# Three layers of attention, retention and gated FFN on one core: a ring of six half-size weight slots, and the modulation vector summed in single steps

## The reference, cut to what matters

```python
# layer 1 (even): differential attention, 8 heads ("A"); gated short conv; cross attention to mem, 4 heads ("X")
u = rms_norm(h, norm_g); proj = u @ e_w_in                      # 1024 x 7168
h = h + concat(ya*silu(az), yb*silu(bz), yx*silu(xz)) @ e_w_out # 2048 x 1024
# layer 2 (odd): forgetting attention, 12 heads ("C"); cross attention, 4 heads ("X")
u = rms_norm(h, norm_g); proj = u @ o_w_in                      # 1024 x 7180
h = h + concat(yc*silu(cz), yx*silu(xz)) @ o_w_out
# layer 3: adaptive modulation, grouped-query attention beside retention, then a gated FFN
mod_x = silu(c) @ w_mod + b_mod      # one vector of 6 * 1024 = 12 chunks of 512
mod_c = silu(c_ctx) @ w_mod + b_mod  # only its first 4 chunks are used
sh_m, sc_m, gt_m, sh_f, sc_f, gt_f = split(mod_x, 6)
hx = rms_norm(x)*(1+sc_m) + sh_m;  hc = rms_norm(ctx)*(1+csc_m) + csh_m
x  = x + gt_m * rms_norm(mix(hx, hc), g_post_mix)
hf = rms_norm(x)*(1+sc_f) + sh_f
x  = x + gt_f * rms_norm(swiglu(hf), g_post_ffn)
```

## Time and profile before

| | |
|---|---|
| median of 3 runs | 1060.45 us (1054.36 to 1062.51) |
| profiled execution, whole | 1062.14 us |
| its span, first to last instruction | 1060.3 us |
| granted TensorE clock over the span | 0.952 of full |
| TensorE busy | 946.7 us (89%) |
| VectorE busy | 702.9 us (66%) |
| ScalarE busy | 475.7 us (45%) |
| GpSimd busy | 66.7 us (6%) |
| moved by DMA | 174.55 MB, 165 GB/s in the mean |

### The profile page before, as it was taken

The page is one execution under the profiler, slowest core; times in us unless marked ns, Lnnn a source line. Parts: engine busy times, 40 slices in busy tenths (PEclk is TensorE's granted clock), DMA queues, the critical chain, the costliest instruction groups (busy, mean ns, idle before and its releaser), DMA issues. The chain is left out here.

```text
span 1060.3 us, 14368 instructions
## 1 busy us (share of the span) xinstructions
PE 946.7 (89%) x5572; PEld 820.6 (77%) x5572; DVE 702.9 (66%) x1058; ACT 475.7 (45%) x800; POOL 66.7 (6%) x63
## 2 busy tenths in 40 slices
PE   4999987999798899999999897987789679999996
PEld 3788866989676778888879676775578579999885
DVE  4567878878777745667686766647745657755643
ACT  4455554544333336555555434434543434333541
POOL 0201110000000010101010000100000000000000
PEclk9999998999899889999999989989999879999999
DMA  7544456665566354545454664341222326663660
GB/s 261 168 150 159 142 177 193 206 225 170 197 216 205 122 187 148 181 158 180 158 187 154 219 227 145 103 158 57 80 80 80 130 89 239 238 199 120 221 215 40
DMA packets 89348, 174.55 MB, mean 165 GB/s; under 512 B 4269, under 2 KB 8770, under 8 KB 89282
## 3 DMA queue, kind: packets, MB, share of 16 engines
q1 hardware_dynamic: 86656, 166.78, 47.1%
q0 software_dynamic: 1888, 6.25, 1.8%
q10 hardware_dynamic: 738, 0.61, 0.2%
HBM read 172.57 MB, written 1.06 MB: 164 GB/s over the span
## 5 line engine op out<-in xcount | busy, mean ns | idle before, releaser
L1570 DVE TENSOR_TENSOR wlo<-raw,whi 128x1024 fp32r<-128x1024 f32 (+2 forms) x278 | 323.5, 1177 | 164.2 <-ACT whi L1287 163.3
L1287 ACT CAST whi<-raw 128x1024 fp32r<-128x1024 f32 (+2 forms) x278 | 276.5, 1010 | 203.6 <-PE acc L987 73.6
L996 PE MATMUL acc<-xhi,whi 128*128 128x256 f32 x736 | 215.1, 292 | 9.6 <-DVE slo L1588 4.5
L997 PE MATMUL acc<-xhi,wlo 128*128 128x256 f32 x736 | 210.1, 285 | 0.0
L998 PE MATMUL acc<-xlo,whi 128*128 128x256 f32 x736 | 210.0, 285 | 0.0
L985 PE MATMUL acc<-whi,xhi 128*128 128x512 f32 (+2 forms) x368 | 151.3, 411 | 11.9 <-DVE xlo L1588 4.6
L996 PEld LDWEIGHTS acc<-xhi,whi 128*128 128x128 f32 x736 | 143.0, 194 | 13.0 <-issue 5.3
L987 PE MATMUL acc<-whi,xlo 128*128 128x512 f32 (+2 forms) x368 | 144.5, 393 | 0.0
L986 PE MATMUL acc<-wlo,xhi 128*128 128x512 f32 (+2 forms) x368 | 144.3, 392 | 0.0
L997 PEld LDWEIGHTS acc<-xhi,wlo 128*128 128x128 f32 x736 | 143.2, 195 | 0.7 <-issue 0.5
L998 PEld LDWEIGHTS acc<-xlo,whi 128*128 128x128 f32 x736 | 143.0, 194 | 0.0
(11 more groups left out here) (291 smaller groups left out, 1179.1 us busy)
## 6 DMA issues: line engine op xcount, KB each, us to landing
raw<-in_e_w_in SPq DMA_DIRECT2D x28, 1024.0 KB, 5.3
raw<-in_o_w_in SPq DMA_DIRECT2D x28, 1024.0 KB, 5.1
raw<-in_w_mod SPq DMA_DIRECT2D x24, 1024.0 KB, 5.1
raw<-in_w_ffn_in SPq DMA_DIRECT2D x20, 1024.0 KB, 5.5
raw<-in_w_in SPq DMA_DIRECT2D x14, 1024.0 KB, 5.2
raw<-in_w_ffn_out SPq DMA_DIRECT2D x10, 1024.0 KB, 5.1
raw<-in_e_w_out SPq DMA_DIRECT2D x8, 1024.0 KB, 6.0
raw<-in_o_w_out SPq DMA_DIRECT2D x8, 1024.0 KB, 5.2
```

The source lines that it names most:

```text
L996: mm(o, wh, hi, start=a, stop=False, skip_group_check=True)
L997: mm(o, wl, hi, start=False, stop=False, skip_group_check=True)
L1287: nc.scalar.copy(whi[:, s.i % SPLIT_SLOTS, 0:s.nk, 0:n], raw[:, s.raw.i % RAW_SLOTS, s.koff:s.koff + s.nk, 0:n]).then_inc(S["hi_ready"], 1)
L1570: tt(wlo[:, slot, 0:s.nk, 0:n], raw[:, s.raw.i % RAW_SLOTS, s.koff:s.koff + s.nk, 0:n], whi[:, slot, 0:s.nk, 0:n].bitcast(F32), ALU.subtra ...
```

## The change

The raw ring becomes six slots of 512 KB instead of three of 1 MB: the same bytes of SBUF, twice the loads, each issued when the load six before it is read. Each k-tile of the modulation is a step of its own. A chunk with `c_ctx` takes one k-tile at every second position (two VectorE instructions), one without it a k-tile at every position (one instruction), both with rank 3, behind all other steps of the position. `mod_out` stands two positions behind the last k-tile, and VectorE's part of it (`mod_take`) one position later, ahead of that position's other steps. The chunks with `c_ctx` (0 to 3) start at position 12 and end at 82, and are followed by none until 100; chunks 4 to 9 are placed from 100 to 148; 10 and 11 stay at 216 to 232. Chunks without `c_ctx` take the halves of `macc` in turn. The gate chunks 4, 5, 10, 11 go the way of the others to columns in `modc`, with the bias from the columns; later (positions 152 to 156, and 236 to 240) VectorE multiplies the identity by the four columns into `macc`, which is the chunk on four diagonals (`gate_diag`), and one matmul of all ones spreads it to all rows of `tp` (`gate_rows`). The bias DMA of GpSimd and the one-row addition are gone.

```diff
-RAWK = 4
-RAW_SLOTS, SPLIT_SLOTS, LEAD = 3, 4, 3
+RAWK = 2
+RAW_SLOTS, SPLIT_SLOTS, LEAD = 6, 4, 3
...
-    def mod(self, pos, chunk, ctx=False, gate=False):
-        pos = max(pos, self.pos) + max(pos, self.pos) % 2
...
+    def mod(self, pos, chunk, ctx=False):
+        pos = max(pos, self.pos)
+        stride = 2 if ctx else 1
+        def read(k):
+            st = self.step("mod", chunk=chunk, u=k // RAWK, part=k % RAWK, ctx=ctx, prev=self.count.get("mod_read", 0),
+                           after=self.count.get("mod_ps", 0))
             self.tick(st, "mod_read")
+            done.append(st.on["mod_read"])
...
+            st = self.step("mod_out", chunk=chunk, ctx=ctx, mod_read=done[-1])
             self.tick(st, "mod_ps", "mod_sb")
-            self.uses(st, "tp" if gate else "o", "mod_sb")
+            self.uses(st, "o", "mod_sb")
             self.chunks.append(chunk)
-        for i in range(4):
-            self.at(pos + (i if ctx else i // 2 * 2), lambda i=i: read(i // 2, i % 2))
-        self.at(pos + 6, out, 2)
-        return pos + 8
+            self.at(self.pos + 1, lambda: self.step("mod_take", first=st), -2)
+        last = pos + (KT - 1) * stride
+        for k in range(KT):
+            self.at(pos + k * stride, lambda k=k: read(k), 3)
+        self.at(last + 2, out, 2)
+        return last + (4 if ctx else 1)
+
+    def gate_row(self, pos, chunk):
...
+        self.at(pos, diag, 2)
+        self.at(pos + 1, rows, 2)
+        return pos + 3
...
     b = heads("A", "g0", evs, pl.pos, 4, 0)
+    m = pl.pos
+    for chunk in range(4):
+        m = pl.mod(m, chunk, ctx=True)
...
-    m = pl.pos
-    for chunk in (6, 7, 8, 9, 0, 1, 2, 3):
-        m = pl.mod(m, chunk, ctx=chunk < 4)
...
     b = heads("X", "g1", evs, pl.pos, 4, 12, gain="ox")
+    m = max(m, pl.pos + 4)
+    for chunk in range(4, 10):
+        m = pl.mod(m, chunk)
...
-    pl.mod(pl.mod(pl.pos + 4, 4, gate=True), 5, gate=True)
+    pl.gate_row(pl.gate_row(pl.pos + 4, 4), 5)
...
-    pl.mod(pl.mod(pl.pos + 8, 10, gate=True), 11, gate=True)
+    m = pl.mod(pl.mod(pl.pos + 8, 10), 11)
+    pl.gate_row(pl.gate_row(m + 4, 10), 11)
...
+            def gate_rows(st):
+                pe.wait_ge(S["gate_diag"], st.on["gate_diag"])
+                wait(st.free["tp"])
+                mm(tp[:, :], ones, macc[:, st.chunk % 2, :], start=True, stop=True).then_inc(S["gate_ps"], 1)
...
             def mod(st):
                 raw_wait(dve, st.raw)
+                wait(("mod_read", st.prev))
+                k = RAWK * st.u + st.part
+                if k == 0:
+                    wait(("mod_ps", st.after))
+                src = raw[:, st.raw.i % RAW_SLOTS, st.part, :]
+                for v in range(2 if st.ctx else 1):
+                    c = scol[:, 8 * v + k:8 * v + k + 1]
+                    m = macc[:, v if st.ctx else st.chunk % 2, :]
+                    if k == 0:
+                        ins = ts(m, src, c, None, ALU.mult)
+                    else:
+                        ins = stt(m, src, c, m, ALU.mult, ALU.add)
+                ins.then_inc(S["mod_read"], 1)
...
+            def gate_diag(st):
+                c = st.chunk
+                wait(("mod_sb", c + 1))
+                d = macc[:, c % 2, :].rearrange("p (i n) -> p i n", i=4)
+                tt(d, ident.unsqueeze(1).to_broadcast([P, 4, P]),
+                   modc[:, 0, 4 * c:4 * c + 4].unsqueeze(2).to_broadcast([P, 4, P]), ALU.mult).then_inc(S["gate_diag"], 1)
...
-            def mod_bias_in(st):
-                wait(("mod_ps", st.prev))
-                pool.dma_start(macc[0:1, 1, :], w["b_mod_2"][:, st.chunk * CW:(st.chunk + 1) * CW])\
-                    .then_inc(S["bias_in"], 16)
```

More of the change, by code:

```diff
@@ L445, in read @@
             self.tick(st, "mod_read")
+            done.append(st.on["mod_read"])
+        done = []
         def out():
[L448 to L453, removed]
+            st = self.step("mod_out", chunk=chunk, ctx=ctx, mod_read=done[-1])
@@ new lines, in mod, with diag, rows @@
+        self.at(last + 2, out, 2)
+        return last + (4 if ctx else 1)
+    def gate_row(self, pos, chunk):
+        pos = max(pos, self.pos)
+        def diag():
+            st = self.step("gate_diag", chunk=chunk)
+            self.tick(st, "gate_diag")
+        def rows():
+            st = self.step("gate_rows", chunk=chunk)
+            st.on["gate_diag"] = self.count["gate_diag"]
+            self.tick(st, "gate_ps", "gate_sb")
+            self.uses(st, "tp", "gate_sb")
+        self.at(pos, diag, 2)
+        self.at(pos + 1, rows, 2)
+        return pos + 3
@@ L648, in make_plan @@
     for c in range(2):
-        pl.panel("w_ffn_out", c * CW, CW, "y", "mix", kts=FFN // P, c=c, which=1, mod_sb=pl.count["mod_sb"])
+        pl.panel("w_ffn_out", c * CW, CW, "y", "mix", kts=FFN // P, c=c, which=1, mod_sb=4)
     st = pl.step("post", sq_ready=pl.count["sq_ready"], v_evac=pl.count["v_evac"])
@@ L755, in finish @@
                 split()
-        if st.kind == "mod" and st.part == 0 and made < n and pl.subs[made].k0 % RAWK:
-            split()
         out.append(st)
@@ L1782, in mod, with mod_take @@
                 raw_wait(dve, st.raw)
[L1783 to L1802 removed]
+                wait(("mod_read", st.prev))
[11 more added lines that the diff above has]
+                ins.then_inc(S["mod_read"], 1)
+            def mod_take(st):
+                st = st.first
                 wait(("mod_ps", st.on["mod_ps"]))
                 c = st.chunk
[L1805 to L1810 removed]
                 for v in range(2 if st.ctx else 1):
@@ L1814, in mod_out, with gate_rows @@
                 last.then_inc(S["mod_sb"], 1)
+            def gate_diag(st):
[4 more added lines that the diff above has]
+                   modc[:, 0, 4 * c:4 * c + 4].unsqueeze(2).to_broadcast([P, 4, P]), ALU.mult).then_inc(S["gate_diag"], 1)
+            def gate_rows(st):
+                c = st.chunk
+                dve.wait_ge(S["loaded_post_ffn" if c >= 6 else "loaded_post_mix"], 16)
+                wait(("gate_ps", st.on["gate_ps"]))
+                g = post_gain[c >= 6][:, (c % 2) * CW:(c % 2 + 1) * CW]
+                tt(g, tp[:, :], g, ALU.mult).then_inc(S["gate_sb"], 1)
             def mod_cols(st):
@@ L1982, in evac_mix @@
                 dve.wait_ge(S["sub_done"], st.done)
-                wait(("mod_sb", st.mod_sb))
+                wait(("gate_sb", st.mod_sb))
                 c = slice(st.c * CW, (st.c + 1) * CW)
@@ L2086, in _ @@
             pool.wait_ge(S["setup_pool"], 1)
-            does = {"forget_sum": forget_sum, "forget_rows": forget_rows, "load": load, "mod_bias_in": mod_bias_in}
+            does = {"forget_sum": forget_sum, "forget_rows": forget_rows, "load": load}
             for st in pl.steps:
@@ L2131 @@
     for n in _ROWS + _HALF_ROWS + _MORE_ROWS + _EVERYWHERE:
-        if n != "b_mod_2":
-            del named[n]
+        del named[n]
     named.update(const_first=first_c, const_ret=ret_c, const_rope=rope_c)
```

46 lines of the change are left out of this document (10 added, 36 removed).

## The result

The changed kernel takes 1053.33 us (median of 15 runs, 1051.44 to 1054.37), the kernel before 1059.64 (median of 15, 1054.36 to 1063.29). The ratio is 0.9944, 95% interval 0.9932 to 0.9956: a gain of 6 us, 0.6%, where 27 was forecast. The time lies inside the range that was given; the gain is under a quarter of the forecast. The profiled execution took 1053.3 us with a span of 1051.5, against 1062.1 and 1060.3 before, so the two traces differ by 8.8 us and their median times by 6.3. The control run of the same kernel (last of the experiments) measured a gain of 0.4%.

The account below looks back on a forecast made before the run. TensorE was taken to bound the kernel where nothing disturbs it, with holes around the modulation. Terms 12 + 11 + 2 + 4 - 6 - 6 + 8 + 2 = 27 us took 1062.1 to 1035; range 1012 to 1056.

Parts of the forecast that it names:

- Positions 64 to 79 and 80 to 95: Modulation halved in the first, nearly gone in the second, fewer load waits: 59.2 to 47 us, 64.3 to 53; gains 12, 11.
- The smaller loads: Twice the loads at 512 KB, fixed part overlapping with up to six under way: 0 us, bounds -2 and +3.
- The rival on transfers: 512 KB loads following each other without overlap bring only 150 GB/s and bind the kernel: above 1090 us, chance 0.03.
- Positions 28 to 43 and 44 to 63: Modulation in pairs behind `oT` shrinks two holes, gain 4; same load but even in the second, gain 2.
- Positions 12 to 27: 12 us of new VectorE work, half filled into idle time: loss 6 us, bounds 0 and 12.
- Positions 100 to 147: 36 us of new VectorE sums, mostly in idle time: loss 3 in 100 to 139, 3 in 140 to 147.
- Positions 152 to 167: Sixteen sums and four 1 MB loads leave; diagonals and gate rows remain: 60.6 to 52-53 us, gain 8.
- Positions 216 to 247: FFN stretch, forecast as 216 to 240: blocks go, four-matmul sums and two gate rows come; gain 2, between -1 and 3.
- half of the new VectorE work on the path: Rival: 18 us paid in 100 to 147, 9 in 12 to 27; 1050, or 1055; both middle cases together 0.16.
- the signs that were to show it: 64 to 79 at 45 to 49 us, 80 to 95 and 152 to 167 some 53, ScalarE's raw-load waits nearly gone.
- the limits that were to warn: Forecast too low if 100 to 147 exceeds 185 us or 12 to 43 exceeds 135.
- VectorE's 120 us in 100 to 139: Sign: VectorE busy 120 us there after the new sums, with the stretch 134 to 138 us long.

Follow-up runs that it names:

- the places alone: Changed kernel put back on the old ring of three 1 MB slots, modulation reads in pairs two positions apart: 1072.92 us, ratio 1.0148 to the kernel before.
- the ring alone: Kernel before with only the ring changed to six slots of 512 KB, modulation left where it was: 1041.87 us, ratio 0.9845.

## Why the prediction was wrong

The direction and the time's range held; the forecast of 27 us did not, and the accounting behind it was wrong. The step that failed is 28 to 63, where the column sums' bank was left out: 6 us of gain forecast, 5.6 of loss measured, 11.6 of the 18 by which the two profiles fall short. In the order of its steps:

- *Positions 64 to 79 and 80 to 95*, 12 and 11 forecast, 13.6 and 8.7 measured. The sizes were near. They were put down to the modulation that leaves and to the ring together; the runs show that either does it alone: 8.5 and 7.2 by the ring, 13.6 and 8.8 by the places.
- *The smaller loads*, taken as 0 beside everything else. As a part by itself this is the change's gain: 15 to 16 us on the old places, and 20 on the new ones (1072.9 against 1053.3). The sum had no place for it. Of the 20, 8.3 are in 100 to 139, 4.7 in 140 to 151 and 3.8 in 12 to 27, stretches for which the forecast counted VectorE's new work and took for granted that the loads arrive in time. So it never asked what the places alone are worth. They are worth less than nothing: 11 us lost on the new ring, 15 on the old. The rival on transfers, with DMAs of 512 KB as the bound, is refuted: with the ring alone 216 to 231 moves 261 GB/s in 512 KB loads, as much as the 259 in 1 MB loads.
- *Positions 28 to 43 and 44 to 63*, gains of 4 and 2 forecast, losses of 0.4 and 5.2 measured. This is the step that failed: it counted VectorE's instructions and never placed `mod_out` and `mod_take`: which bank they write, who holds it there, what stands behind them on TensorE. In the kernel before the sums of the A heads stood at 34, 42 and 50, three positions behind a `pv`, and only the first held the next `pv`, by 1.5 us. The change puts chunk 0's one position behind a `pv`, and has all of them taken a position later, behind VectorE's work. The two waits of 7.3 and 2.6 us and the low clock behind them are what the runs showed in place of the gain. With the sums moved off the bank's use the two stretches take 142.5 and 146.1 us in two executions, around the 144.4 that the forecast makes of them (150.4 less 6). The prediction named two bank waits for the gate rows and none for these.
- *Positions 12 to 27*, 6 forecast, 3.3 measured. VectorE's busy time rose by 7.0 us, not 12. TensorE was idle 3.0 us, not the 5 to 8 that were named as the sign.
- *Positions 100 to 147*, 3 and 3 forecast. The first is 3.8, but for another reason than given: not VectorE's sums, which cost nothing measurable there, but TensorE's matmuls, which had been priced at 0.5 us a chunk for the FFN from two overlapping records and left out here. A chunk's four cost 0.95 us. The second is 6.4, and 2.6 more in 148 to 151, which the forecast left out though the last chunk's sum stands in it. The term of 3 us took four of eight reads on the path, no late load and no clock; the stretch lost more than the reads' full 5.7 us.
- *Positions 152 to 167*, 8 forecast, 8.2 measured; the ring alone gives 0.5 there, the places on the old ring 8.8. Right, with its mechanism.
- *Positions 216 to 247*, 2 forecast, a loss of 0.9. 216 to 231 gained 3.3 as the blocks went; behind it one column sum, two gate rows and a wait of 1.4 us for a diagonal behind the panel's end took 4.2. Two positions between diagonal and row took 1.7 of that back.

Of the rivals, half of the new VectorE work on the path gave 1050 to 1055, and there the time came out, but by luck: the mechanism holds at most in 140 to 151, 12 to 27 lost less than the forecast and not more, and the larger part of the shortfall is the bank and the column sums, which no rival named. Of the signs that were to show it, 64 to 79, 152 to 167 and ScalarE's waits came as said, and 80 to 95 took 55.6 us where some 53 were; 12 to 43 (132.5 us) and 100 to 147 (178.1) stayed inside the limits that were to warn. The limits were blind to 44 to 63 and 148 to 151. VectorE's 120 us in 100 to 139 came out at 111.5: 39 more instructions, most of 749 ns, added 21.0 us of busy time, since busy time counts the overlap of two neighbours once.

The Trainium skill (DMA: Bandwidth & Descriptors, Rules for kernel authors) wants 1 MiB or more per DMA for full bandwidth. Here halving the loads at the same buffer space made the kernel 1.6% faster and moved 261 GB/s where the large ones moved 259, so for such a ring, with several loads under way, the measurement decides, and it does not bear the rule out. The fit of 2.0 us that the prediction took from the page is given there for DMAs issued from GpSimd; these loads are issued from SyncE. The page's remark that the fixed part is hidden when a DMA is issued early agrees with this case, though no run here measures the fixed part by itself.

## What to carry to other kernels

Test the parts of a change one by one before pricing the whole: here one part was worth 1.6%, and the other took some two thirds of it back. When work moves to another place in an in-order schedule, price first what it waits for and who stands behind it (bank, semaphore, the engine's next instruction), and only then its duration; eight matmuls of 0.24 us each cost 7 us of TensorE and the clock behind it by standing one position behind the bank's last user; one position later it was 2.7 us. Spare time of an engine belongs to a stretch: the same sums cost VectorE's side nothing in 100 to 139 and 158 to 165, and beside the context's norm, with their loads, 6.4 us for 5.7.

## What the runs showed of the hardware

- Loads of 512 KB in six slots carry as much as loads of 1 MB in three: 261 against 259 GB/s in the FFN's first 16 subs. The median from issue to landing was 3.5 us for the four `w_ffn_in` loads of that size in the kernel before. By tensor it was 3.6 to 4.7 with the ring alone and 3.7 to 5.7 in the changed kernel, with six slots in both; two of the latter's tensors:

```profile
raw<-in_o_w_in SPq DMA_DIRECT2D x56, 512.0 KB, 5.4
raw<-in_w_mod SPq DMA_DIRECT2D x48, 512.0 KB, 4.3
```

- A column sum is cheap in arithmetic and not in time. Each of its matmuls moves one column, and still takes 0.24 us of TensorE in a running stream (2.9 us for twelve). Its two weight-load records are 209 ns long in the mean over both clock levels. The group of the 64 such matmuls in the changed kernel (busy us, mean ns, idle before):

```profile
L1107 PEld LDWEIGHTS opsum<-cst,macc 128*128 128x128 f32 x128 | 17.3, 209 | 10.7 <-issue 7.5 <-DVE macc L1812 2.7
```

So the sum of one chunk, four matmuls, costs 0.95 us where TensorE has no idle time, a third of a sub.
